# Four-layer transformer stack on one core: order of the out projections and of some low parts

## What is computed

```python
x = x + even_mixer(rms_norm(x, g), ...)        # layer 1: attention, then y @ w_out
x = x + squared_relu_mlp(rms_norm(x, g), ...)
x = x + odd_mixer(rms_norm(x, g), ...)         # layer 2: attention, then y @ w_out
x = x + squared_relu_mlp(rms_norm(x, g), ...)
x = x + mlstm_mixer(rmsnorm(x, g), ...)        # layer 3: x_in, z; heads; normalise; @ w_out
x = x + nsa_mixer(rmsnorm(x, g), ...)          # layer 4
return rmsnorm(x, final_norm)

# even and odd mixer, end:   einsum("bse,ed->bsd", y, w_out)     y: 256 x 1024
# mlstm mixer, end:          ((hn + skip * x_conv) * silu(z)) @ w_out
```

## Time and profile before

| what | us |
|---|---|
| median of 3 runs | 1002.1 (1001.03 to 1003.13) |
| the profiled execution's own time | 1001.25 |
| its span, first to last instruction | 999.5 |
| PE busy in the span | 961.9 (96%) |
| DVE busy | 634.9 (64%) |
| ACT busy | 556.7 (56%) |
| POOL busy | 137.3 (14%) |

### The profile page before, as it was taken

How to read it: one execution, slowest core, us unless ns; L and a number is a source line. 1 busy time by engine, 2 the same in 40 slices (tenths; PEclk the granted TensorE clock), 3 DMA queues, 4 the chain that set the end, 5 groups by cost and what they waited for, 6 DMA issues and landing times.

```text
span 999.5 us, 14211 instructions
## 1 busy us (share of the span) xinstructions
PE 961.9 (96%) x5636; PEld 808.8 (81%) x5636; DVE 634.9 (64%) x1136; ACT 556.7 (56%) x918; POOL 137.3 (14%) x170
## 2 busy tenths in 40 slices
PE   6998999999999999999999999999998999999997
PEld 4865788888888777688888888999986899988875
DVE  4866777773446455568775354874677566477782
ACT  6685564543434666655454343654685446377771
POOL 0556000000000000000000034343013001211100
PEclk9999999999999999999999999999999999999999
DMA  9722444555454424136555564234332643321101
GB/s 356 259 85 85 168 166 173 192 186 209 171 198 146 161 85 169 47 132 227 186 178 201 198 218 169 95 129 157 128 111 93 237 159 135 128 86 61 68 22 42
DMA packets 21922, 150.30 MB, mean 150 GB/s; under 512 B 2528, under 2 KB 2656, under 8 KB 4448
## 3 DMA queue, kind: packets, MB, share of 16 engines
q1 hardware_dynamic: 21856, 149.40, 42.2%
HBM read 148.35 MB, written 1.05 MB: 149 GB/s over the span
## 4 chain that ended last, share of the span: by engine, by line
PE 83%; DVE 7%; ACT 7%; issue 2%; DMA 0%; SPq 0%; ACTq 0%; DVEq 0%
PE bank L191 17%; PE bank L193 16%; PE bank L192 16%; PE bank L1165 12%; PE bank L1166 6%; ACT w_hi L157 2%; DVE w_lo L161 2%; PE bank L931 2%; PE bank L2283 1%; PE bank L2292 1%; PE bank L944 1%; PE bank L763 1%; PE bank L1606 1%; PE bank L2307 1%; PE bank L1591 1%
## 5 line engine op out<-in xcount | busy, mean ns | idle before, releaser
L161 DVE TENSOR_TENSOR w_lo<-raw,w_hi 128x2048 fp32r<-128x2048 f32 x122 | 280.8, 2303 | 147.2 <-ACT w_hi L157 147.1
L157 ACT ACTIVATE w_hi<-raw 128x2048 fp32r<-128x2048 f32 x136 | 259.4, 1911 | 114.1 <-PE bank L193 114.1
L1165 PE MATMUL bank<-h,w_hi 128*128 128x512 f32 x512 | 181.2, 396 | 0.0
L1166 PE MATMUL bank<-h,w_lo 128*128 128x256 f32 x512 | 144.4, 282 | 0.0
L191 PE MATMUL bank<-h,w_hi 128*128 128x256 f32 x448 | 129.6, 289 | 0.7 <-DVE nsa_kcv L2630 0.7
L192 PE MATMUL bank<-h,w_hi 128*128 128x256 f32 x448 | 125.2, 279 | 0.0
L193 PE MATMUL bank<-h,w_lo 128*128 128x256 f32 x448 | 125.0, 279 | 0.0
L1165 PEld LDWEIGHTS bank<-h,w_hi 128*128 128x128 f32 x512 | 96.2, 188 | 23.3
L191 PE MATMUL bank<-w_hi,mlp_u_hi 128*128 128x512 f32 x256 | 101.0, 395 | 0.0
L193 PE MATMUL bank<-w_hi,mlp_u_lo 128*128 128x512 f32 x256 | 100.4, 392 | 0.0
L192 PE MATMUL bank<-w_lo,mlp_u_hi 128*128 128x512 f32 x256 | 99.4, 388 | 0.0
(11 more groups left out here) (388 smaller groups left out, 1658.8 us busy)
## 6 DMA issues: line engine op xcount, KB each, us to landing
raw<-in_chunks SPq DMA_DIRECT2D x136, 1024.0 KB, 4.8
xres<-in_x SPq DMA_DIRECT2D x2, 512.0 KB, 5.4
raw<-in_chunks SPq DMA_DIRECT2D x2, 512.0 KB, 6.8
out<-final_xn SPq DMA_DIRECT2D x2, 512.0 KB, 2.6
ml_z<-in_ml SPq DMA_DIRECT2D x1, 896.0 KB, 6.2
even_const<-in_even SPq DMA_DIRECT2D x1, 576.0 KB, 15.0
small<-in_small SPq DMA_DIRECT2D x1, 559.5 KB, 12.9
final_gain<-in_fnorm SPq DMA_DIRECT2D x1, 512.0 KB, 3.6
```

The source lines that it names most:

```text
L157: act.activation(w_hi[slot][:, :], raw[slot][:, :], ACT.Copy).then_inc(hi_ready, 1)
L161: dve.tensor_tensor(w_lo[slot][:, :], raw[slot][:, :], w_hi[slot][:, :].bitcast(F32), ALU.subtract).then_inc(lo_ready, 1)
L1165: pe.matmul(dst[:, :], w_hi[slot][:, cols], h[:, k, :, :], start=(k == 0), stop=False)
L1166: last = pe.matmul(dst[:, 0:S], w_lo[slot][:, cols], h[:, k, 0, :], start=False, stop=(k == KT - 1))
```

## The change

Four edits, all of them in the order of instructions; none is added or taken away.

1. PE, `OutPhase.pe`, first chunk of both layers 1 and 2: the half of row tile 1 with the near pairs changes places with the half of row tile 0 with the far pairs. Both row tiles of pairs 0 and 1 are now computed ahead of `turn(4)` and `score(5)`, and both of pairs 2 and 3 behind them.
2. DVE, `OutPhase.dve`, layers 1 and 2: `low(7)` goes ahead of the low part of a whole weight chunk (`rest_for(c0 + 2)`).
3. ACT, layer 3's end: `root(1)` goes ahead of the high part of a weight chunk (`round_for(c0 + 15)`).
4. DVE, same place: the low part of that chunk (`rest_for(c0 + 15)`) goes ahead of four `keep_low`.

```diff
@@ OutPhase.pe
             self.half(pe, 0, 0, near, True, False)
             att.values(pe, 3)
-            self.half(pe, 0, 0, far, False, False)
+            self.half(pe, 0, 1, near, True, False)
             att.turn(pe, 4)
             att.score(pe, 5)
-            self.half(pe, 0, 1, near, True, False)
+            self.half(pe, 0, 0, far, False, False)
             att.values(pe, 4)
             self.half(pe, 0, 1, far, False, False).then_inc(chunk_used, 1)
@@ OutPhase.dve
             for c, half in after:
                 rest_half(dve, c, half)
+            att.low(dve, 7)
             rest_for(dve, c0 + 2)
-            att.low(dve, 7)
             self.add(dve, 0)
@@ Mlstm.act
             self.silu_z(act, 6)
+            self.root(act, 1)
             round_for(act, c0 + 15)
-            self.root(act, 1)
             self.normal(act, 2)
@@ Mlstm.dve
             self.normals(dve, 1)
+            rest_for(dve, c0 + 15)
             self.keep_low(dve, 0, 1)
             self.keep_low(dve, 1, 1)
-            rest_for(dve, c0 + 15)
             self.keep_z(dve, 7)
```

## The result

| | us |
|---|---|
| before, median of 6 runs | 1001.87 (999.57 to 1003.13) |
| changed, median of 6 runs | 994.81 (992.61 to 995.44) |
| ratio | 0.9923, 95% interval 0.9912 to 0.9934 |
| profiled execution of the changed kernel: own time, span | 995.35, 993.4 |

The change makes the kernel 7.1 us faster by the medians and 7.7 us by the ratio (6.6 to 8.8). The prediction said 6.4 us less, and 995.7 us as the time.

The account below looks back on a forecast made before the run. The prediction took PE, busy 961.9 of 999.5 us, as the bound. Its terms, 2.4 + 0.9 + 2.0 + 1.1 = 6.4 us, gave 994.85 us for the profiled execution, 995.7 as median; own range 994.3 to 997.1.

Parts of the forecast that it names:

- Edit 1, layer 1: PE's first chunk in layer 1: 1.1 us idle time saved, 1.7 clock, less 0.4 beside POOL, together 2.4 us.
- The term of 1.7 us: Layer 1, behind PE's stall: the shorter stall was to keep the clock at 2.4 GHz, saving 1.7 us (bounds 0 and 1.7).
- The loss beside POOL: Layer 1, turn(5): DVE work moved earlier is slowed beside POOL, so PE waits 0.4 us (bounds 0 and 1.4).
- Edit 1, layer 2: PE's first chunk in layer 2: the break of 0.79 + 0.15 us goes whole, 0.9 us.
- Edit 2: Out phases of layers 1 and 2: PE's second wait on y_lo goes in each, 2 x 1.0 = 2.0 us.
- Layer 3's end: Layer 3's end: DVE's idle times of 0.72 and 0.38 us go, PE's out projection starts 1.1 us earlier (bounds 0.7 and 1.2).
- The sum: 6.4: Whole kernel: gains of 2.4 + 0.9 + 2.0 + 1.1 = 6.4 us, none lost again later.
- the falling clock: Rival, layer 1: the clock falls behind the remaining stall all the same, 1.7 us not won, 997.2 us; chance 0.17.
- the idle edit 1: Rival, layers 1 and 2: the waits only move to score(5) and turn(5), 3.3 us lost, 999.0 us; chance 0.05.
- layer 3 without effect: Rival, layer 3's end: DVE waits for ACT's later weight chunk or normal, nothing gained, 996.8 us; chance 0.10.
- More is won: Rival: no loss beside POOL and a low-clock stretch goes elsewhere too, 0.4 + 1.7 us less, 993.6 us; chance 0.07.
- The slower rival: Rival, whole kernel: the shift puts five new 1.2 GHz stretches behind gaps that had none, 1004 us; chance 0.03.

Follow-up runs that it names:

- e5_long_stall: All four edits, with DVE's second half chunk in layer 1 moved from pair 5 to pair 4, ahead of scale(4); median 993.43 us, ratio 0.9927.
- e6_no_bias67: All four edits, but POOL builds the attention biases of layer 1's pairs 6 and 7 for one column only; median 991.47 us, ratio 0.9901.
- e1_pe_swap: The kernel before with only the PE order changed in the first chunk of layers 1 and 2; median 995.74 us, ratio 0.9946.
- e9_both: All four edits plus e8_z_first's change and DVE's layer 1 half chunks each one place later; 989.38 us, ratio 0.9886.
- e8_z_first: All four edits, but at layer 3's end DVE does keep_z(7) first, then keep_low, two mixes, then the weight chunk's low part; 987.73 us, ratio 0.9866.

## Why the prediction was right

The time was forecast as 995.7 us and came out as 994.81, inside the forecast's own range of 994.3 to 997.1. By its steps:

- **Edit 1, layer 1: 2.4 us, measured 2.3.** The old wait gave way to one for `scale(4)`: 1.4 us were forecast, 1.30 are there. `score(5)`'s own wait for `low(3)` was covered. The sum counted 0.15 us of lost overlap for the break that goes and none for the one that stays, so that it had 1.1 us of idle time where the two waits differ by 1.0. The clock stayed at full speed behind the stall. The reason given for it, that a shorter stall leaves the clock alone, was not confirmed: e5_long_stall had a longer one and kept it as well. The term of 1.7 us was right for this place (none of nine profiles has a stretch there, five of five had one before), but its reason is not shown, and by that much its size is luck.
- **The loss beside POOL: 0.4 us, measured 0.3** (96.03 against 95.50 + 0.24). The size was right and the split was not: the half chunk was not slowed (1.22 us), `scale(5)` took 1.55 in place of 1.01. It came as one blocked instruction, not in proportion: the first of `scale(5)`'s four operations took 0.83 us in place of 0.29 and ended together with an instruction of POOL. That POOL costs the remaining stall too was not in the forecast; e6_no_bias67 showed it.
- **Edit 1, layer 2: 0.9, measured 1.05. Edit 2: 2.0, measured 1.19 + 1.09 = 2.3.** No wait is left in either place. The terms were a little small because the price of a break was: besides 0.15 us of lost overlap, the first matmul behind a wait takes 0.34 us to the next start and not 0.24, 0.1 us more for each of the breaks. In the timeline of before, behind the wait of the earlier trace rows, it reads:

```profile
402.50 0.50 PE L191 MATMUL bank<-w_hi,odd_y_hi 128*128 128x512 f32 x1 [0.79 <-DVE odd_y_lo L1023]
402.84 0.39 PE L192 MATMUL bank<-w_lo,odd_y_hi 128*128 128x512 f32 x1
403.07 0.39 PE L193 MATMUL bank<-w_hi,odd_y_lo 128*128 128x512 f32 x1
```

- **Layer 3's end: 1.1, measured 1.16.** Both idle times of DVE went, and the cover of the later weight chunk held. The split 0.72 and 0.38 was 0.58 and 0.47 in the runs, since edit 3 alone makes `normal` 0.1 us late. One sign named in advance did not come: PE's wait for `ml_z` was to be 2.8 us and is 3.3. PE starts as much earlier as forecast, but it also reaches its wait 0.5 us earlier, since the transposes ahead of it (L1660) wait less for the normalised values; the 0.3 us that they stood for ACT's are gone.
- **The sum: 6.4, by the trace 6.8, by the medians 7.1, by the ratio 7.7.** The part at full clock was forecast as 6.4 - 1.7 = 4.7 us and is 4.9; the clock was forecast as 1.7 and is 2.1, within a little over its error of 0.35. That it came so near is in part luck, since the forecast took the stretches elsewhere to stay as they are, and they do not: e1_pe_swap alone lost 3.7 us less. None of the idle time saved was given back later.

Of the rivals, the falling clock (in the nine profiles with the new order), the idle edit 1 and layer 3 without effect are ruled out by the traces. *More is won* had a true half: stretches of lower clock come and go elsewhere when the program shifts. e1_pe_swap lost 3.7 us less to the clock, where its own place accounts for 1.7. The slower rival was built on the same effect. No kernel of this study lost more to the clock than before, but a shift of the program can add to the loss: all four edits lost 1.6 us more than edit 1 alone (7.4 and 5.8), and e9_both 2.2 us more than e8_z_first.

## What to carry to other kernels

When an engine waits, look at what stands between the waited-for instruction and the moment its inputs were there: an independent piece of work that is needed later belongs behind it, and the wait that comes next in line gives the true gain. Work that is not needed for another 11 us, like layer 3's weight chunk, should not stand ahead of the instruction that the bounding engine waits for at all; e8_z_first won another 4.4 us at that place, 2.8 of them at the wait itself, where the change won 1.2. A piece that fills another wait, like the half chunk while ACT makes the exp, brings nothing by being moved away.

## What the runs showed of the hardware

- The lower clock is no fixed cost. The same instructions had none, 3.4 or 6.8 us of it in different profiles, and e8_z_first, 2.6 us under the changed kernel at full clock, is 6.1 us under it in time. Span times mean clock, over several executions, separated the two to within 0.8 us of what the traces show.
- A stall of 2.3 us in layer 1 had the lower clock behind it in five of five profiles, at once or up to 1.3 us later; one of 2.4 us at nearly the same place had not in its one profile, with PE equally idle ahead of it. A stall of 3.3 to 3.9 us in layer 3 had it in 12 of 12.
- POOL and DVE can block each other for whole instructions: an operation of POOL on one column, 0.21 us alone, took 1.26 us behind one of DVE's, and an operation of DVE's `scale(5)`, 0.29 us alone, took 0.83 behind one of POOL's.
